# 64 instead of 32 tokens leave the dense expert stages; scatter takes two picks an instruction, for two halves of blocks; DVE adds value rows

## The reference

```python
q = (xt @ w_q).reshape(T, PEER_HEADS, 2, PEER_HALF)
s = einsum('thpd,hpkd->thpk', q, sub_keys)
sv, si = lax.top_k(s, 16)                                # per head and half
cand = sv[:, :, 0, :, None] + sv[:, :, 1, None, :]
top, f = lax.top_k(cand.reshape(T, 8, 256), 16)
experts = i1 * 128 + i2                                  # 8 x 16 a token
gates = softmax(top, axis=-1)
h = gelu(einsum('tkd,td->tk', u[experts], x))
out = einsum('tk,tkd->td', gates * h, v[experts])
x = x + gt2 * out
```

## Time and profile before

| | us |
|---|---|
| median of three runs | 2760.04 |
| profiled execution | 2767.51 |
| its span in the trace | 2765.7 |
| PE busy | 2662.2 (96%) |
| DVE busy | 2050.5 (74%) |
| ACT busy | 1332.8 (48%) |
| POOL busy | 813.2 (29%) |
| hidden stage, layer 0 | 322.9 to 886.0 |
| output stage, layer 0 | 886.0 to 1397.0 |
| hidden stage, layer 1 | 1678.4 to 2237.6 |
| output stage, layer 1 | 2237.6 to 2748.4 |

### The profile page before, as it was taken

How to read it: one execution, slowest core, us unless ns; L and a number is a source line. 1 busy time by engine, 2 the same in 40 slices (tenths; PEclk the granted TensorE clock), 3 DMA queues, 4 the chain that set the end, 5 groups by cost and what they waited for, 6 DMA issues and landing times.

```text
span 2765.7 us, 45861 instructions
## 1 busy us (share of the span) xinstructions
PE 2662.2 (96%) x16908; PEld 2598.5 (94%) x16908; DVE 2050.5 (74%) x4116; ACT 1332.8 (48%) x2509; POOL 813.2 (29%) x536
## 2 busy tenths in 40 slices
PE   7999999999999899999999899999999989999998
PEld 6979999999999899999998799998999989999998
DVE  3535686999895599999865457779988846677765
ACT  3444543356375444444444454433745734444443
POOL 0010008677700133333201000377765001222220
PEclk8999999999999999999999899999999999999999
DMA  7383359857947989898644124797587497777772
GB/s 301 131 313 129 126 177 348 238 144 182 269 143 256 353 305 343 321 336 324 253 157 151 60 103 164 270 298 205 127 242 208 152 335 276 264 272 268 259 271 78
DMA packets 274517, 632.86 MB, mean 229 GB/s; under 512 B 43888, under 2 KB 208112, under 8 KB 229296
## 3 DMA queue, kind: packets, MB, share of 16 engines
q1 hardware_dynamic: 218880, 517.29, 53.9%
q0 software_dynamic: 55472, 113.44, 13.6%
HBM read 535.59 MB, written 94.99 MB: 228 GB/s over the span
## 4 chain that ended last, share of the span: by engine, by line
PE 65%; DVE 22%; DMA 5%; issue 3%; SPq 2%; ACT 2%; POOL 0%; POOLq 0%; ACTq 0%; DVEq 0%
PE ps L1018 21%; PE ps L959 21%; PE ps L809 11%; DVE v_lo L1865 5%; DVE u_lo L1649 3%; DVE mod_p L1915 3%; DMA act_scratch<-act_h 3%; PE ps L831 2%; DVE w L1871 2%; PE ps L983 2%; DVE w_lo L1875 1%; SPq L498 1%; PE ps L920 1%; PE ps L989 1%; PE ps L754 1%
## 5 line engine op out<-in xcount | busy, mean ns | idle before, releaser
L959 PE MATMUL ps<-h_lo,u_hi 128*128 128x352 f32 x2048 | 667.5, 326 | 30.0 <-DVE u_lo L1649 28.7
L1018 PE MATMUL ps<-w_hi,v_lo 128*128 128x352 f32 (+1 forms) x2048 | 663.9, 324 | 23.0 <-DVE v_lo L1865 22.9
L1018 PE MATMUL ps<-w_lo,v_hi 128*128 128x352 f32 x2048 | 664.7, 325 | 0.0
L1018 PE MATMUL ps<-w_hi,v_hi 128*128 128x352 f32 x2048 | 663.3, 324 | 0.0
L959 PE MATMUL ps<-h_hi,u_hi 128*128 128x352 f32 x2048 | 662.6, 324 | 0.0
L959 PE MATMUL ps<-h_hi,u_lo 128*128 128x352 f32 x2048 | 662.3, 323 | 0.0
L1865 DVE TENSOR_TENSOR v_lo<-wring,v_hi 128x512 fp32r<-128x512 f32 x512 | 435.2, 850 | 186.4 <-ACT v_hi L1304 186.2
L706 POOL DMA_INDIRECT gate_scratch<-scat_g,scat_i x256 | 439.5, 1717 | 154.2 <-issue 100.9
L1304 ACT CAST v_hi<-wring 128x512 fp32r<-128x512 f32 x512 | 308.9, 617 | 269.0 <-PE ps L1018 268.7
L959 PEld LDWEIGHTS ps<-h_lo,u_hi 128*128 128x128 f32 x2048 | 386.6, 189 | 43.1 <-DVE u_lo L1649 41.8
L1649 DVE TENSOR_TENSOR u_lo<-wring,u_hi 128x1024 fp32r<-128x1024 f32 x256 | 312.9, 1222 | 153.1 <-ACT u_hi L1236 150.4
(11 more groups left out here) (265 smaller groups left out, 3670.1 us busy)
## 6 DMA issues: line engine op xcount, KB each, us to landing
wring<-in_u_t_dram SPq DMA_DIRECT2D x128, 1024.0 KB, 5.7
wring<-in_v_t_dram SPq DMA_DIRECT2D x128, 1024.0 KB, 5.7
act_scratch<-act_h SPq DMA_DIRECT2D x256, 176.0 KB, 5.9
gate<-gate_scratch SPq DMA_DIRECT2D x64, 704.0 KB, 6.3
act<-act_scratch SPq DMA_DIRECT2D x64, 704.0 KB, 8.5
gate_scratch<-g_all SPq DMA_DIRECT2D x32, 1024.0 KB, 8.1
wring<-in_w_ada_dram SPq DMA_DIRECT2D x24, 1024.0 KB, 6.3
mod_w<-in_w_mod_dram POOLq DMA_DIRECT2D x24, 1024.0 KB, 7.2
```

Source lines behind the costliest of these rows:

```text
L959: last = nc.tensor.matmul(ps[:, 6 + s % 2, 0:TD], u[:, s % 2, k], hx[:, k, 0:TD], start=(k == 0 and n == 0), stop=(k == KC - 1 and n == 2))
L1018: last = nc.tensor.matmul(ps[:, half * (KC // 2) + c, cols], v[:, of % 4, d], w[:, group * G + of, cols], start=(opening and k == 0), stop ...
```

## The change

1. `NS` = 64: the dense stages work on `TD` = 320 tokens instead of 352, and 64 tokens' picks are gathered row by row (`SLOTS` = 64 a layer instead of 32).
2. Scatter: half of block 0 (64 tokens) and half of block 1 are scattered. Two picks go into one instruction of 128 partitions, so there are again 128 scatters a layer, in two halves; POOL waits after every 8. DVE stages the cells (`cells_staged`), POOL moves them across partitions by two small DMAs a half (`cells_in_two`).
3. So block 1 has 8 gate steps and not 16, and 24 lead steps and not 16.
4. The last block's 8 gate pieces are issued by ACT, all at once after its gate steps.
5. Value rows: DVE scales and adds a row in one instruction, every 3 units; POOL and ACT do nothing for them.
6. `v_hi`, `v_lo` are made 1024 columns at a time, w and its halves two blocks at a time.
7. The sums of squares of three of the norms (not the first): POOL adds the 8 blocks of squares, and PE needs one matmul for 8.

```diff
-NS = 32
+NS = 64
+HALF = P // 2
+PICKS2 = PH * TOPK // 2
-LEAD_STEPS = (0, 16, 0)
+LEAD_STEPS = (0, 24, 0)
+GATE_FIRST = (16, 8, 0)
+GATE_STEPS = tuple(16 - first for first in GATE_FIRST)
-ROUTE_DOTS = tuple(int(s % 2 == 1 and s < 18) + 2 * (s in (21, 22)) for s in range(TOPK_STEPS))
+ROUTE_DOTS = tuple(1 + (s % 4 == 3) + (s in (20, 21, 22)) if s < 23 else 0 for s in range(TOPK_STEPS))
-V_FIRST, V_EVERY, V_AHEAD = 24, 7, 10
+V_FIRST, V_EVERY, V_AHEAD = 24, 3, 10
...
+        def squares_added(N):
+            pool.wait_ge(sq_rdy.sem, N * KC + 1)
+            for k in range(1, KC):
+                pool.wait_ge(sq_rdy.sem, N * KC + (k + 1))
+                if k > 1:
+                    pool.wait_ge(sa_rdy.sem, (N - 1) * (KC - 1) + (k - 1))
+                nc.gpsimd.tensor_tensor(h[:, 0], h[:, 0], h[:, k], ALU.add).then_inc(sa_rdy.sem, 1)
...
+            for half in range(2):
+                cells_in_two(half)
+                for j in range(PICKS2):
+                    if j and j % (TOPK // 2) == 0:
+                        pool.wait_ge(sc_st.sem, sc_st.at(l, 16 * (half * PICKS2 + j)))
+                    if half == 0 and U_RING + 2 * j < SLOTS:
+                        picked_rows(l, U_RING + 2 * j)
+                        picked_rows(l, U_RING + 2 * j + 1)
+                    add_gates(half, j)
...
+                if tb + 1 == TB:
+                    act.wait_ge(tq_evac.sem, tq_evac.at(l, NQ))
+                    act.wait_ge(gq_evac.sem, gq_evac.at(l, NQ))
+                    for piece in range(PIECES):
+                        keys = slice(piece * (NK // PIECES), (piece + 1) * (NK // PIECES))
+                        act.dma_start(gate_dram[keys, :, ORDER[tb] * P:(ORDER[tb] + 1) * P].rearrange("a b t -> b a t"), g_all[:, keys]) \
+                            .then_inc(g_st[piece].sem, 16)
...
+            def expert_row(s):
+                b, pair = s % V_RING, vr_ld[s // 2 % V_PAIRS]
+                dve.wait_ge(pair.sem, pair.at(l, 32 * (s // V_RING + 1)))
+                ...
+                    V.scalar_tensor_tensor(acc_s[:], v_rows_s[:, b], w_s[:, s:s + 1], acc_s[:], ALU.mult, ALU.add) \
+                        .then_inc(as_rdy.sem, 1)
```

More of the change, by code:

```diff
@@ L258, in build @@
     act_dram = nc.dram_tensor("act_scratch", (NB, P, T), F32).ap()
+    scat_u, scat_v = [scat[:, half, 0] for half in range(2)], [scat[:, half, 1] for half in range(2)]
     gate_cells = gate_dram.rearrange("a b (t o) -> (a b t) o", o=1)
@@ L263, in build @@
     iota = cst[:, C_IOTA:C_IOTA + P]
-    token = cst[:, C_TOK:C_TOK + 1]
+    token = [cst[:, C_TOK + half:C_TOK + half + 1] for half in range(2)]
     def S(name, per, credit=0):
@@ L336, in build @@
     pk_evac = S("pk_evac", GT)
-    NQ = GT * GATE_STEPS
+    NQ = sum(GATE_STEPS)
     one_rdy = S("one_rdy", NQ)
@@ L748, in _, with sums @@
             pe.sem_inc(sig.sem, sig.credit)
-        def sums(N, blocks):
-            for k in blocks:
-                pe.wait_ge(sq_rdy.sem, N * KC + (k + 1))
-                last = nc.tensor.matmul(ps[:, sum_bank(N), 0:T], ones, h[:, k], start=(k == 0), stop=(k == KC - 1))
-                if k == KC - 1:
-                    last.then_inc(sum_mm.sem, 1)
+        def sums(N):
+            if N == 0:
+                for k in range(KC):
+                    pe.wait_ge(sq_rdy.sem, k + 1)
+                    last = nc.tensor.matmul(ps[:, sum_bank(N), 0:T], ones, h[:, k], start=(k == 0), stop=(k == KC - 1))
+            else:
+                pe.wait_ge(sa_rdy.sem, N * (KC - 1))
+                last = nc.tensor.matmul(ps[:, sum_bank(N), 0:T], ones, h[:, 0], start=True, stop=True)
+            last.then_inc(sum_mm.sem, 1)
         pe.wait_ge(const_ld.sem, 16)
@@ L761, in _ @@
             if l == 0:
-                sums(0, range(KC))
+                sums(0)
             def tile_in(n):
@@ L841, in queries @@
                     scaled_columns(SP_WQ0 + m, pq_bank(m), k, 1, g2_hi, g2_lo, pq_mm)
-                    if m == 0 and k >= KC - 2:
-                        sums(2 * l + 1, (k,))
+                if m == 0:
+                    sums(2 * l + 1)
             def values_turned(i):
@@ L855, in _ @@
             else:
-                for k in range(KC):
-                    scaled_columns(0, pj_bank(0), k, 0, g1_hi, g1_lo, pj_mm)
-                    if k == 0:
-                        pe.wait_ge(xa_evac.sem, xa_evac.at(l, sum_bank(2 * l) + 1 - KC))
-                    sums(2 * l, (k,))
+                projection(0)
+                pe.wait_ge(xa_evac.sem, xa_evac.at(l, sum_bank(2 * l) + 1 - KC))
+                sums(2 * l)
             for m in range(1, 2 * N_IN):
@@ L1895, in unit_step @@
             def unit_step(i, n, last_units):
-                next_w = n % 2 == 0 and not (last_units and n >= 2 * G)
+                next_w = n % 4 == 0 and not (last_units and n >= 2 * G)
                 b = n // 2 + G
```

249 lines of the change are left out of this document (129 added, 120 removed).

## The result

The changed kernel takes 2742.87 us (median of 8 runs, 2737.76 to 2745.64) against 2760.55 us (8 runs, 2756.23 to 2775.44) of the kernel before on the same chip: ratio 0.9926, 95% interval 0.9913 to 0.994. Predicted were 2688 us and a range of 2628 to 2732. The sign was right, the size was not: 18 us of the 72.

What follows compares the result with a forecast made beforehand. PE bounds the output stage, DVE routing and gates of block 1; -13 (sums) - 9.3 (hidden) + 2 x 19 - 2 x 14.7 - 41.7 - 17.5 = -72.9, taken as -72 from 2760.0: 2688 us, range 2628 to 2732.

Steps and rivals of the forecast that it cites:

- Price of a matmul: PE's matmuls of 320 columns: 146.5 ns each, a step 3.52 instead of 3.87 us, a unit 1.76 instead of 1.923.
- output units: Output stages: layer 1 gains 256 x 0.163 = 41.7 us; layer 0 gains 6.1 and 11.4 us.
- DVE's load in layer 0: Layer 0's output stage: with modulation DVE needs 1.85 to 1.87 us a unit from unit 27 to 213, more than PE.
- Routing and gates: Hidden stage: block 1's routing 123.5 us and 8 gate steps 41.3 us, block 2's routing 91.5 us.
- ACT's hold by its stores: End of hidden stage: eight stores hold ACT 25 us, PE idles 24.7, eight steps take 55.2 instead of 36.4, +19 a layer.
- rival 1: End of hidden stage: ACT isn't held by its stores, PE keeps 27 us a layer, 2634 us; chance 18%.
- Scatters, "hidden, with 41 us in hand": POOL's scatters beside the steps end at 416 us after the picks are known; ACT looks for them at 457.
- rival 3: Before the last 8 hidden steps: scatters end late, ACT waits; slower than before once POOL is 36 us late a layer; 7%.
- Lead steps, 95 us: Block 1's 24 lead steps: 84.5 us at PE's pace, a row every 2.1 us, DMAs full, dots behind: 95 us.
- Sums of squares, -13: Three norms: POOL adds the squares, PE loses 7 of 8 sum matmuls, 13.6 us, taken as -13.
- up to 5 us would go: Norms' sums: if the doubled clearing DMAs run late in layer 0, up to 5 of the 13.6 us would go.
- Rival 2: DMAs bound more than PE and DVE: lead steps 102 us, layer 0's output about 2.0 us a unit; 2722 us; 18%.

Runs made afterwards that it cites:

- e12: e7's kernel with DVE's modulation products in layer 0's output stage over 512 of 1024 elements, DMAs kept; ratio 0.974 to the kernel before.
- e2: Changed kernel with the last block's gate stores back in SP's list, three pieces ahead of the loads, five behind; ratio 0.9992 to the kernel before.
- e7: Changed kernel with e3's and e4's edits together: clears in two parts, staging DMAs ahead of the gathers; 2709.51 us, ratio 0.98 to the kernel before.
- e9: e7's kernel with each gather of u rows moving 256 KB instead of 512 KB, DVE's time kept; ratio 0.9755 to the kernel before.
- e10: e7's kernel with three gathers instead of two ahead of each of the first six scatters, then 5 in 3; ratio 0.9796 to the kernel before.
- e11: e7's kernel with 28 instead of 33 dots in the lead steps, 36 instead of 31 in block 1's routing; ratio 0.9821 to the kernel before.
- e14: e7's kernel with the lead's 33 dots beginning at step 5 instead of 2; ratio 0.9801 to the kernel before.
- e3: Changed kernel with the clearing DMAs split, block 1's half moved behind the second norm's sum; ratio 0.9892 to the kernel before.
- e4: Changed kernel with the first half's staging DMAs ahead of the 16 gathers, scatter-batch waits behind the next two gathers; ratio 0.9839 to the kernel before.
- e6: Changed kernel without 32 of the second half's 64 scatters, and ACT's gate stores one behind each of the last eight casts; ratio 0.9832 to the kernel before.
- e5: Changed kernel with 32 of the second half's 64 scatters left out in each layer; ratio 0.991 to the kernel before.

## Why the prediction was off, by its steps

- *Price of a matmul, output units, DVE's load in layer 0* held: 145.8 ns; 477.9 and 458.1 us for 479 and some 455. e12 shows that DVE was the bound of layer 0's output stage, as argued.
- *Routing and gates* held: 122.8 us (123.5 predicted), 39.8 (41.3), 93.0 (91.5).
- *ACT's hold by its stores* held in size, against rival 1: 20.1 us more for the eight steps in layer 0 and, with the scatters, 25.2 in layer 1, where 19 were predicted (before, they took 36.4 and 35.2 us). That the total of this term fits in layer 0 is partly luck: with the stores on SP PE stands 26 us there too (e2), so the same 19 us would have been paid without the move. The scatters below were the second cause.
- *Scatters, "hidden, with 41 us in hand"* failed. From the known picks to the last scatter it took 472 us (412.7 to 884.5), not 416, and ACT was done with its gate steps at 451 (863.6), not 457. From the picks to the end of the staging it took 44.5 us (412.75 to 457.29), not 35, and a scatter was counted at 1.41 + 0.30 = 1.71 us; its mean was 1985 ns, 2.29 with the 0.30: for the 104 behind the last gather 60 us more, of which shorter parts elsewhere gave some back. Timeline of POOL beside gate steps, and right behind the last of them:

```profile
856.43 2.55 POOL L721 DMA_INDIRECT gate_scratch<-scat  x1 [0.30 <-issue]
...
862.04 1.55 POOL L721 DMA_INDIRECT gate_scratch<-scat  x1 [0.30 <-issue]
```

  In the changed kernel that shows only as 2.9 us in layer 1, since ACT's eight stores stand ahead of its wait for the scatters. The sum and rival 3 didn't see that: by the kernel's own order the scatters had another 25 us in hand.
- *Lead steps, 95 us* failed: 108.7 and 107.6. This term alone is 26 us of the 50: it is the step of the prediction that failed most. I counted a row every 2.1 us. POOL's wait for the staging DMAs was in the schedule of the scatters, and not in that of the rows, though the same list issues both: 14.5 us without a gather, then 7.3 more for the first 8 scatters. With the order changed (e7) the steps take 98.6 and 98.0. Of the 14 us left over PE's pace 5 go with half of the rows' bytes (e9); e10, e11 and e14 don't find the other 9, and their cause stays open.
- *Sums of squares, -13* failed: -7 to -10 for the sums, +8.8 for the clears, in all -1 to +2 (+2.4 in the two profiled executions). The bound "up to 5 us would go" for late clears was too small: POOL is held 35 us by its own 16 DMAs, which had cost nothing while no other engine waited for POOL. e3 gives it back.

Rival 2's first half (lead steps at 102 us) comes nearer to the measured 108.7 than the forecast. The trace alone doesn't refute it: 345 GB/s at a share of 0.96, where before it was 346 at 0.97. But e4 takes 6.0 and 8.6 us off with the same bytes in another order, so the bytes weren't the limit at 345 GB/s; the rows were asked for late. Rival 3's mechanism was there, 23 us late of the 36 a layer that it needed, and hidden.

How much of e4's 24 us comes from the staging and how much from the batch wait behind the gathers wasn't separated.

## What to carry to other kernels

In this kernel POOL's stalls cost nothing until others waited for it. When an engine gets work that others wait for (POOL's sums, POOL's staging), first list what already stands in its list ahead of that work; they are now on the path. A small DMA behind large ones on the same queue can cost the large ones' time (here 14.5 us), so try issuing it first. And where two waits end together, undoing one shows nothing: the price of each only comes out with the other taken away.

## What the runs showed of the hardware

- Eight stores of 1 MB held ACT's queue 25.9 us in one go, and 34.9 us one at a time under full DMAs (e6). Issued singly they held it between 0.38 and 10.32 us each, so issuing them apart is no remedy by itself. The Trainium skill ("DMA: Bandwidth & Descriptors", section "Issuing engines are not separate DMA queues") speaks of the sequencer's time as usually small relative to the DMA; here it was 25.9 us of ACT and PE's 26.6.
- An indirect scatter from 128 partitions took 1.55 us alone and 2.55 beside the gate steps; a gather of 512 KB mostly 0.94 us, in the changed kernel's lead and routing steps up to 2.69.
- The DMAs moved 383 (changed kernel) and 393 GB/s (e12) for 300 us in a row.
- Between the expert stages the same instructions took 270.2 us in e5 and 277.4 in e7. The granted clock in the attention stage differs (77 us of e5, then of e7), after the same projections on PE and in no relation to the edits that shows here. The 14 kernels with POOL's sums fall into groups by it: 270.1 to 271.0 us at 0.91 (5 of them), 273.2 to 274.9 at 0.87 (4), 274.0 to 277.6 at 0.82 or 0.83 (5). Why one execution gets the higher share of 2.4 GHz stays open.

```profile
1471.80:1549.10 77.30, 66.76 (x356) 53.19 (x355) 35.56 (x108) 40.42 (x116) 19.74 (x18) 0.91 0.58 130
```

```profile
1456.40:1533.40 77.00, 68.06 (x335) 54.23 (x334) 35.31 (x103) 37.58 (x106) 10.54 (x10) 0.83 0.35 87
```
